# First block's rotary positions: a partition shuffle on VectorE in place of products with a rotation matrix

## The reference

```
def partial_rope(x, cos, sin):
    half = ROT_DIM // 2                      # ROT_DIM = 16
    x1, x2, xp = x[..., :half], x[..., half:ROT_DIM], x[..., ROT_DIM:]
    return jnp.concatenate([x1 * c - x2 * s, x1 * s + x2 * c, xp], axis=-1)

# layer 0 (even mixer): 4 heads x 2 components, a causal difference attention
q = partial_rope(...) * (DA_HEAD_DIM ** -0.5);  k = partial_rope(...)
# layer 1 (odd mixer): 16 heads, dilated attention
q = partial_rope(heads(q), cos, sin) * (DL_HEAD_DIM ** -0.5);  k = partial_rope(heads(k), cos, sin)
```

## Time and profile before

| what | value |
|---|---|
| median of 3 runs | 1855.76 us (1855.68 to 1857.1) |
| span of the profiled execution | 1854.1 us (the page gives no other time of its own; the median lies 1.7 us above the span) |
| TensorE busy | 1788.8 us, 96% |
| VectorE busy | 1275.2 us, 69% |
| ScalarE busy | 990.7 us, 53% |
| transfers | 334.92 MB, mean 181 GB/s |

### The profile page before, as it was taken

One profiled execution on the slowest core, in us unless ns is written; L12 is line 12 of the kernel. 1 busy time (PEld: TensorE's weight loads), 2 busy tenths in 40 slices (PEclk: granted clock), 3 DMA queues, 4 the chain that ended last, 5 costly groups with the idle time before them and its releaser, 6 DMA issues. The chain is left out here.

```text
span 1854.1 us, 35690 instructions
## 1 busy us (share of the span) xinstructions
PE 1788.8 (96%) x14792; PEld 1663.2 (90%) x14792; DVE 1275.2 (69%) x2351; ACT 990.7 (53%) x1741; POOL 76.2 (4%) x78
## 2 busy tenths in 40 slices
PE   7999999999999999999889999999999999989997
PEld 6778899978888999999889988899999898679997
DVE  5566656568778755886766777765676867876665
ACT  4565545466556544654755655554455555644443
POOL 0000100020000200000100101000000000100000
PEclk9999999999999999999999999999999999989999
DMA  9797865676344555455454443455655543236663
GB/s 377 273 354 253 325 184 190 185 291 195 122 117 140 165 185 185 126 171 182 128 174 155 149 159 93 150 178 184 186 177 193 162 137 107 86 114 185 184 186 120
DMA packets 93825, 334.92 MB, mean 181 GB/s; under 512 B 10960, under 2 KB 12880, under 8 KB 93536
## 3 DMA queue, kind: packets, MB, share of 16 engines
q1 hardware_dynamic: 92016, 327.33, 54.1%
q0 software_dynamic: 1648, 5.31, 0.9%
HBM read 331.55 MB, written 1.05 MB: 179 GB/s over the span
## 5 line engine op out<-in xcount | busy, mean ns | idle before, releaser
L565 DVE TENSOR_TENSOR low<-ring,high 128x1024 fp32r<-128x1024 f32 x410 | 500.8, 1223 | 218.4 <-ACT high L557 209.0
L590 PE MATMUL bank<-XHx,high 128*128 128x256 f32 x2096 | 608.7, 290 | 21.9 <-DVE low L565 9.7
L591 PE MATMUL bank<-XLx,high 128*128 128x256 f32 x2096 | 592.2, 283 | 0.0
L592 PE MATMUL bank<-XHx,low 128*128 128x256 f32 x2096 | 591.0, 282 | 0.0
L557 ACT CAST high<-ring 128x1024 fp32r<-128x1024 f32 x410 | 428.6, 1045 | 276.0 <-PE bank L592 230.5
L590 PEld LDWEIGHTS bank<-XHx,high 128*128 128x128 f32 x2096 | 397.6, 190 | 41.3 <-issue 9.7
L591 PEld LDWEIGHTS bank<-XLx,high 128*128 128x128 f32 x2096 | 398.1, 190 | 1.5 <-issue 0.2
L592 PEld LDWEIGHTS bank<-XHx,low 128*128 128x128 f32 x2096 | 398.2, 190 | 0.0
L590 PE MATMUL bank<-XHc,high_side 128*128 128x256 f32 x608 | 180.9, 297 | 10.2 <-DVE low_side L565 8.1
L591 PE MATMUL bank<-XLc,high_side 128*128 128x256 f32 x608 | 172.0, 283 | 0.0
L592 PE MATMUL bank<-XHc,low_side 128*128 128x256 f32 x608 | 171.7, 282 | 0.0
(11 more groups left out here) (448 smaller groups left out, 3052.1 us busy)
## 6 DMA issues: line engine op xcount, KB each, us to landing
ring<-in_stream SPq DMA_DIRECT2D x410, 512.0 KB, 3.7
ring_side<-in_stream SPq DMA_DIRECT2D x110, 512.0 KB, 3.7
ring_mod<-in_stream SPq DMA_DIRECT2D x96, 512.0 KB, 8.0
x_nb<-in_rpb POOLq DMA_DIRECT2D x6, 256.0 KB, 3.1
x_late_NB<-in_rpb POOLq DMA_DIRECT2D x6, 256.0 KB, 3.1
Xx<-in_x SPq DMA_DIRECT2D x2, 512.0 KB, 5.8
Xc<-in_ctx SPq DMA_DIRECT2D x1, 1024.0 KB, 7.0
out<-y SPq DMA_DIRECT2D x8, 128.0 KB, 2.0
```

Source lines behind the costliest of these rows:

```text
L565: nc.vector.tensor_tensor(st.low[:, j % st.n_ring, :], st.ring[:, j % st.n_ring, :], st.high[:, j % st.n_split, :].bitcast(F32), ALU.subtr ...
L590: nc.tensor.matmul(out, wh, xh, start=(i == 0), stop=False)
L591: nc.tensor.matmul(out, wh, xl, start=False, stop=False)
L592: m = nc.tensor.matmul(out, wl, xh, start=False, stop=(c == ks[-1]))
```

## The change

For the first block's two layers, `tensor_rope` with `rot1` is taken away and VectorE does the exchange of features itself. One shuffle gives every partition the value of another partition of the same group of 32: partitions 0 to 7 get 8 to 15, partitions 8 to 15 get 0 to 7, and 16 to 31 keep their own. (In the second 32 features of each head the sines are zero.) The signs that stood in the matrix now stand in the sine table. The constant `rot1` (64 KB) is no longer loaded or kept in SBUF. The second block still goes by `tensor_rope` with `rot2`.

```
-ROPE_CONSTS = ["cos1", "sin1", "rot1"]
+ROPE_CONSTS = ["cos1", "sin1"]
-    out["rot1"], out["rot2"] = rotation(8), rotation(32)
+    out["rot2"] = rotation(32)
-    out["sin1"] = np.where(rot, np.sin(ang1)[:, d % 8].T, 0.0)
+    out["sin1"] = np.where(rot, np.sin(ang1)[:, d % 8].T, 0.0) * np.where(d < 8, -1.0, 1.0)[:, None]
...
+EXCHANGED = [*range(8, 16), *range(8), *range(16, 32)]
+
+def vector_exchange_rope(k, w, tag, chunks, cos, sin):
+    nc, V = k.nc, k.V
+    for i, dst in chunks:
+        V.wait_ge(k.s_copied, (yield tag, "copied", i))
+        j = yield from w.tmp.take(V, (tag, "rope", i))
+        tmp = w.TMP[:, j, :]
+        nc.vector.stream_shuffle(tmp, dst, EXCHANGED).then_inc(*V.tick(k.s_vec, V_us(SEQ), (tag, "exchanged", i)))
+        V.wait_ge(k.s_vec, V.last)
+        V.wait_ge(k.s_start, (yield "constants"))
+        nc.vector.tensor_tensor(tmp, tmp, sin, ALU.mult).then_inc(*V.tick(k.s_vec, V_us(SEQ)))
+        nc.vector.tensor_tensor(dst, dst, cos, ALU.mult).then_inc(*V.tick(k.s_vec, V_us(SEQ)))
+        V.wait_ge(k.s_vec, V.last)
+        nc.vector.tensor_tensor(dst, dst, tmp, ALU.add).then_inc(*V.tick(k.s_vec, V_us(SEQ), (tag, "rope", i)))
+        yield None
...
-    k.add(T, tensor_rope(k, x, "ev", qk, k.c["rot1"][:, :]), 0)
-    k.add(V, vector_rope(k, x, "ev", qk, k.c["cos1"][:, :], k.c["sin1"][:, :]), 1)
+    k.add(V, vector_exchange_rope(k, x, "ev", qk, k.c["cos1"][:, :], k.c["sin1"][:, :]), 1)
...
-            k.add(T, tensor_rope(k, x, "od", qk, k.c["rot1"][:, :]), 0)
-            k.add(V, vector_rope(k, x, "od", qk, k.c["cos1"][:, :], k.c["sin1"][:, :]), 1)
+            k.add(V, vector_exchange_rope(k, x, "od", qk, k.c["cos1"][:, :], k.c["sin1"][:, :]), 1)
```

More of the change, by code:

```diff
@@ L1039, in vector_store_low, with tensor_rope @@
                 *V.tick(k.s_xl, V_us(SEQ), (tag, "stored", i), name(u["to"])))
-def tensor_rope(k, w, tag, chunks, rot, source=None):
+def tensor_rope(k, w, tag, chunks, rot, source):
     nc, T = k.nc, k.T
     for i, dst in chunks:
-        T.wait_ge(k.s_copied, (yield source or tag, "copied", i))
-        T.wait_for((yield "loaded", "rot1" if source is None else "rot2"))
+        T.wait_ge(k.s_copied, (yield source, "copied", i))
+        T.wait_for((yield "loaded", "rot2"))
         b = yield from w.banks.take(T, (tag, "sin", i))
```

## The result

The changed kernel takes 1869.63 us (median of 4 runs, 1864.69 to 1873.43) against 1856.43 us before (1855.68 to 1858.21): ratio 1.0078, 95% interval 1.0059 to 1.0097. It is slower by some 13 us; the forecast was 1847.6 us with a range up to 1857, so it was wrong in its sign.

A forecast was written before the change was run, and what follows sets the result against it. TensorE, busy 96% of the span, was taken as the bound. Gains of 5.4 (odd stage), 2.5 (even stage) and 0.3 us (start) sum to 8.2, giving 1847.6 us; range 1839 to 1857, the forecast's own 1842 to 1852.

The forecast's parts named there:

- What leaves TensorE: Even and odd layers of the first block: 24 rope products at 0.43 us each leave TensorE, 10.3 us.
- What VectorE gets: Each rotary chunk costs VectorE 0.45 us more for the shuffle and its wait, bounds 0.34 and 0.73; 10.8 us in all.
- Given back in the odd stage, 1.5 us: Odd layer: of 6.9 us leaving TensorE, 1.5 are lost to a full VectorE, bounds 0 and 5; gain 5.4 us.
- the even layer: Even stage: 3.4 us of ropes leave, 0.9 lost to tile transfers; gain 2.5 us, bounds 2.1 and 3.4.
- Break-even of the shuffle, 1.3 us: Odd stage: VectorE's spare time, (91 - 69.7) / 16, would be used up at 1.3 us per shuffle.
- Start, 0.3 us: Kernel start: SyncE no longer issues rot1, 0.43 us, so later transfers go out sooner; 0.3 us counted as gain.
- Everything behind: Rest of the kernel, newly ordered: zero gain or loss, with a spread of one long wait, 8.5 us either way.
- VectorE takes the odd stage: Rival, odd layer: shuffle with wait costs 0.73 us, loss 5 instead of 1.5; 1851.1 us, up to 1855; chance 0.16.
- A long wait more: Rival, 900 to 1000 us or like boundary: late `low_side` tile and low clock, 1856.1 us; chance 0.10, two 0.06.
- slower 0.10: Chance of a whole-kernel time above 1859.5 us, from two long waits more and some of the single one.

The follow-up runs named there:

- run 1: Kernel before, its instruction order kept, with the 24 rope products replaced by 24 shuffles and rot1 still loaded: 1844.7 us against 1854.26, ratio 0.9949.
- run 12: Shuffles in place of rope products in the order of the kernel before, without the load of rot1: 1842.81 us against 1855.42, ratio 0.9931.
- Run 8: Order of the kernel before, rope products replaced by three shuffles in a row per chunk, each waiting for the one before: 1861.37 us, ratio 1.0036.
- run 2: Kernel before with its rope products, planned with costs like the changed kernel's (rope product 0, sine multiplication doubled), so another order: 1877.67 us against 1854.26, ratio 1.0131.
- run 3: Changed kernel with shuffles in the even layer alone; the odd layer keeps its rope products: 1861.68 us, ratio 1.0042 against the kernel before.
- run 4: Changed kernel with shuffles in the odd layer alone; the even layer keeps its rope products: 1870.71 us, ratio 1.0087 against the kernel before.
- run 5: Kernel before with the planner's delay on VectorE results 0.13 instead of 0.12 us, so only the order changes: 1863.38 us against 1854.6, ratio 1.0045.
- run 6: Changed kernel with the planner's delay on VectorE results 0.13 instead of 0.12 us: 1864.96 us, ratio 1.0050 against the kernel before.
- run 7: Changed kernel whose planner counts nothing for a shuffle, though the chip still does it: 1870.57 us, ratio 1.0081 against the kernel before.
- run 11: Changed kernel with the planner's delay on TensorE results 0.23 instead of 0.25 us: 1862.93 us, ratio 1.0035 against the kernel before.
- run 10: Changed kernel's order to the instruction, with the 24 shuffles left out and the sines multiplying the chunk itself: 1869.72 us, ratio 1.0071 against the kernel before.
- run 9: Kernel before with planner's VectorE delay 0.13 instead of 0.12 us, that order kept, rope products replaced by shuffles: 1852.1 us, ratio 0.9979 against the kernel before.

## Why the prediction was wrong

**What leaves TensorE: right.** 24 x 0.43 = 10.3 us were forecast; the two comparisons in one order gave 9.6 and 11 (12.6 with the load of rot1 gone too). These are differences of whole kernels, so what waits changed by is in them.

**What VectorE gets: right.** 0.48 us per chunk against 0.45 forecast.

**Given back in the odd stage, 1.5 us: next to nothing was.** With VectorE nearly as full as the forecast feared (81.7 of 91 us in run 1) TensorE waited 2 us in 454 to 560 us, where before it waited 1.0. The first `odd_q` came at 452.3 instead of 455.1: the even layer brought 2.8 us by then (2.5 forecast). Behind the odd layer's attention the lower half of the same weight tile was begun at 609.4 instead of 619.0 us: 6.8 us more, nearly all of the 6.9 that left. By the first `x_gla_gk` (967.4 instead of 974.8) 2.2 of them were gone again, in stretches that the forecast had left at zero.

**Break-even of the shuffle, 1.3 us: probably too high.** Run 8 shows that at about 1.4 the loss is already 6.8 us, and the line between runs 1 and 8 crosses at about 1.0. The sum of VectorE's room over a stage counted gaps that no chunk can use, because the scores wait for their chunk (L859 behind L1086, 5.8 us in 7 waits).

**Start, 0.3 us: right in kind.** TensorE's wait at 20.39 ended at 19.96 in the changed kernel, 0.43 us sooner, and at 19.76 in run 12. One execution of each is profiled, and run 1, with rot1 loaded, ended it at 20.5.

**The step that failed: "Everything behind. The other work is the same, but its order is laid anew. I put zero on that, with a spread."** It measured some 27 us: the changed kernel's 1869.6 against 1842.8 for the same work in the old order (run 12). Three things were wrong in it. I priced the order as one long wait more or less, between 900 and 1000 us. But the waits for `low_side` in that stretch went down (6.6 us against 10.2), and the loss is spread over the whole span; among it are waits of 1.5 to 4.4 us at about 150, 500, 523, 552 and 1215 us, and the low clock behind some of them. I also held that a short wait costs only itself. But in this window of the changed kernel, with waits of 1.5 and 0.9 us in it, the granted clock was 0.72 of full speed:

```profile
520.00:530.00 10.00, 7.44 (x43) 6.59 (x42) 9.14 (x20) 2.54 (x8) 0.00 (x0) 0.72 0.18 52
```

And I took the order of before for one of many alike, as likely to be replaced by a better as by a worse one. All seven newly laid orders that ran (runs 2 to 7 and 11) were slower than before, and so was the changed kernel, although six of the eight carry less work for TensorE. Among these nine orders that of before is the best. Why it is so good, and which property of an order costs the time, stays open; that it was picked among many is a guess.

**The rivals.** "VectorE takes the odd stage" did not happen (runs 1 and 10). "A long wait more" had the right sign and the right parts, waits and low clock, but a wrong size, place and chance: I gave slower 0.10.

## What to carry to other kernels

Where a planner or a list scheduler lays out the order, an edit changes two things at once: the work, and the order of everything behind it. Measure them apart: keep the old order with phantom costs (the planner still counts what is no longer issued) and put the new work in, and run the old work with a nudge of the planner that changes nothing else. If a nudge moves the time by more than the edit is worth, a forecast needs the order's spread in its range, and an order that has been measured as good should be held fixed or searched again, not left to whatever falls out of the edit.

## What the runs showed of the hardware

**Shuffle.** 0.444 us for 128x256 float32, with an instruction of 0.014 us before it for the choice of lanes. The prediction's estimate from the Trainium skill, "VectorE: DVE Perf Modes", perf-mode tier table, was 0.53 us. It was too high because it added the whole difference of 107 ns, which stands there at 2048 elements, to a shuffle of 256; an eighth of it, 13 ns, would have given an estimate of 0.43. The measured shuffle takes 0.03 us more than the tensor_tensor of the same shape (0.42) behind it. That the lane choice is loaded by an instruction of its own (the Trainium skill, "Vector Engine (DVE) Microarchitecture Reference", section 3.8) is what the trace shows, before each of the 24.

**Clock.** The same order and nearly the same waits gave different granted clocks. In these windows of the changed kernel and then of run 10, TensorE was idle for the same 2.1 us, yet the mean granted clock of the 20 us was 0.91 in the first and 1.00 in the second:

```profile
490.00:510.00 20.00, 17.91 (x138) 16.03 (x139) 15.47 (x46) 10.40 (x26) 0.00 (x0) 0.91 0.41 134
```

```profile
490.00:510.00 20.00, 17.91 (x151) 15.89 (x149) 15.13 (x43) 11.82 (x28) 0.00 (x0) 1.00 0.43 135
```

The changed kernel's own runs lie 8.7 us apart, 1864.69 us at a mean clock of 0.989 and 1873.43 at 0.983; 0.006 x 1870 = 11 us is about that. So one order's executions can differ by several us with the clock. That this order is less steady than others isn't shown: the four executions of run 10, in the same order, lie 2.5 us apart, and the 19 of the kernel before beside runs 9 to 12 lie 6.6 us apart.
